# Relative-position bias rows: one product with eight output partitions, copied 128 times by the transfer to DRAM

## The reference

```python
bias = rel_bias[t5_bucket(sel_pos - q_pos[None, :, None])]
logits = logits + jnp.moveaxis(bias, 3, 1).astype(jnp.float32)
logits = jnp.where(valid[:, None], logits, -jnp.inf)
p = jax.nn.softmax(logits, axis=-1)
```

## Time and profile before

| | |
|---|---|
| three runs | 1038.37, 1040.26, 1038.22 us, median 1038.37 |
| profiled execution | span 1036.2 us from its first to its last instruction |
| TensorE busy | 1004.3 us, 97% |
| ScalarE, VectorE, GpSimd busy | 489.1, 621.5, 494.4 us |
| granted TensorE clock, mean | 0.996 of full |

### The profile page before, as it was taken

One profiled execution on the slowest core, in us unless ns is written; L12 is line 12 of the kernel. 1 busy time (PEld: TensorE's weight loads), 2 busy tenths in 40 slices (PEclk: granted clock), 3 DMA queues, 4 the chain that ended last, 5 costly groups with the idle time before them and its releaser, 6 DMA issues.

```text
span 1036.2 us, 18753 instructions
## 1 busy us (share of the span) xinstructions
PE 1004.3 (97%) x7590; PEld 921.0 (89%) x7590; DVE 621.5 (60%) x1221; ACT 489.1 (47%) x843; POOL 494.4 (48%) x331
## 2 busy tenths in 40 slices
PE   6999999999999999999999999899999999999996
PEld 5878997888899999997788899787888999999975
DVE  7579996879953200450765899978898320110137
ACT  6565336658866322222136633466788542222220
POOL 2425554535656534546324265555455464544540
PEclk9999999999999999999999999999999999999998
DMA  7521532101211425223243124301111222342312
GB/s 238 182 75 60 195 116 87 42 1 46 77 44 51 142 85 189 85 83 122 93 148 115 42 94 127 128 2 43 42 42 42 83 82 82 116 149 82 121 42 91
DMA packets 70105, 95.44 MB, mean 92 GB/s; under 512 B 4474, under 2 KB 61284, under 8 KB 69380
## 3 DMA queue, kind: packets, MB, share of 16 engines
q1 hardware_dynamic: 66068, 82.68, 23.9%
q0 software_dynamic: 3776, 11.50, 3.2%
q10 hardware_dynamic: 176, 0.07, 0.0%
HBM read 79.47 MB, written 14.78 MB: 91 GB/s over the span
## 4 chain that ended last, share of the span: by engine, by line
PE 81%; DVE 14%; issue 2%; ACT 2%; DMA 0%; POOL 0%; DVEq 0%; ACTq 0%; POOLq 0%
PE ps L559 36%; PE ps L915 10%; PE ps L866 10%; DVE attn L1520 3%; PE ps L781 3%; DVE top L1517 3%; PE ps L583 3%; PE ps L802 2%; PE ps L683 2%; PE ps L841 2%; PE ps L820 2%; PE ps L760 2%; PE ps L664 2%; PE ps L607 1%; DVE attn L1555 1%
## 5 line engine op out<-in xcount | busy, mean ns | idle before, releaser
L1759 POOL TENSOR_TENSOR w_lo<-raw,w_hi 128x1024 fp32r<-128x1024 f32 x115 | 282.0, 2452 | 390.3 <-ACT w_hi L966 390.1
L559 PE MATMUL ps<-xT_hi,w_hi 128*128 128x288 f32 x864 | 256.1, 296 | 0.0
L559 PE MATMUL ps<-xT_hi,w_lo 128*128 128x288 f32 x864 | 254.5, 295 | 0.0
L559 PE MATMUL ps<-xT_lo,w_hi 128*128 128x288 f32 x864 | 254.4, 294 | 0.0
L966 ACT ACTIVATE w_hi<-raw 128x1024 fp32r<-128x1024 f32 (+1 forms) x116 | 121.3, 1047 | 110.2 <-PE ps L559 71.2
L559 PEld LDWEIGHTS ps<-xT_hi,w_hi 128*128 128x128 f32 x864 | 162.1, 188 | 1.3 <-issue 1.1
L559 PEld LDWEIGHTS ps<-xT_lo,w_hi 128*128 128x128 f32 x864 | 162.1, 188 | 0.0
L559 PEld LDWEIGHTS ps<-xT_hi,w_lo 128*128 128x128 f32 x864 | 162.1, 188 | 0.0
L1720 DVE TENSOR_TENSOR qy<-qy,ps 128x576 f32<-128x576 f32 x32 | 24.1, 754 | 203.9 <-PE ps L559 203.9
L1074 ACT ACTIVATE qy<-ps,bias 128x576 f32<-128x576 f32 x33 | 24.5, 744 | 126.2 <-PE ps L559 126.1
L1851 POOL TENSOR_TENSOR attn<-attn 128x1024 f32<-128x1024 f32 (+1 forms) x24 | 54.2, 2260 | 59.1 <-DVE attn L1628 59.1
(11 more groups left out here) (227 smaller groups left out, 2327.1 us busy)
## 6 DMA issues: line engine op xcount, KB each, us to landing
raw<-in_w_in SPq DMA_DIRECT2D x44, 1024.0 KB, 4.9
raw<-in_w_out SPq DMA_DIRECT2D x8, 1024.0 KB, 4.9
x_kept<-x_nat SPq DMA_DIRECT2D x2, 2560.0 KB, 11.1
x_nat<-x_kept SPq DMA_DIRECT2D x2, 2560.0 KB, 11.8
raw<-in_w_proj_a SPq DMA_DIRECT2D x8, 512.0 KB, 3.5
raw<-in_w_proj_b SPq DMA_DIRECT2D x8, 512.0 KB, 4.5
x_nat<-in_x_prompt SPq DMA_DIRECT2D x4, 512.0 KB, 5.4
out<-stage POOLq DMA_DIRECT2D x8, 256.0 KB, 4.6
```

Of the source, the lines that this page charges most:

```text
L559: last = mm(out, a, b[:, HALF * half:HALF * (half + 1)], start=(k == 0 and i == 0), stop=(k == n - 1 and i == 2))
L1759: g.tensor_tensor(lo, src, hi.bitcast(f32), ALU.subtract).then_inc(s_lo, 1)
```

## The change

The table `rel_bias` itself (32 buckets by 8 heads) becomes the stationary operand. One product gives 8 partitions, one for each head, of 384 distances; the factor -1 goes into the one-hot matrix, on the host. `rel_wide`, its eight VectorE operations and its semaphore go, seven of the eight products and of the copies too. TensorE waits for the one copy where it waited for eight. The write to `scratch` reads the 8 partitions with a step of zero over 128 copies, so that `scratch` holds what it held before; it stands at the same place in SP's order.

```diff
@@ views
-        rows = view(r0, NH, REL)
+        rows = view(r0, REL)
-        rel_wide = stage[:, :, :].rearrange("p a n -> p (a n)")[:, 0:1024].rearrange("p (h n) -> p h n", h=NH)
@@ sync
                     if L == 0 and CHUNKS[c][0:2] == ("VA", 0):
-                        sp.wait_ge(s_relc, NH)
-                        sp.dma_start(scratch, rows[:, :, :]).then_inc(s_reld, 16)
+                        sp.wait_ge(s_relc, 1)
+                        of = rows[0:NH, :]
+                        sp.dma_start(scratch.rearrange("p h r -> h p r"),
+                                     bass.AP(of.tensor, of.offset, [list(of.ap[0]), [0, 128], [1, REL]])).then_inc(s_reld, 16)
@@ tensor
-            def rel_rows(h0):
-
-                if h0 == 0:
-                    pe.wait_ge(s_relw, NH)
-                    pe.wait_ge(s_trev, 1)
-                else:
-                    pe.wait_ge(s_relc, h0)
-                for h in range(h0, h0 + 4):
-                    mm(ps[:, 4 + h % 4, 0:REL], rel_wide[0:N_BUCKETS, h, :], onehot[0:N_BUCKETS, :],
-                       start=True, stop=True).then_inc(s_relp, 1)
+            def rel_rows():
+
+                pe.wait_ge(s_rel, 32)
+                pe.wait_ge(s_trev, 1)
+                mm(ps[0:NH, 4, 0:REL], rel_in[0:N_BUCKETS, :], onehot[0:N_BUCKETS, :],
+                   start=True, stop=True).then_inc(s_relp, 1)
...
-                    if L == 0 and u in (8, 9):
-                        rel_rows(4 * (u - 8))
+                    if L == 0 and u == 8:
+                        rel_rows()
                     if L == 0 and u == 10:
-                        pe.wait_ge(s_relc, NH)
+                        pe.wait_ge(s_relc, 1)
@@ scalar
-                    if L == 0 and u in (8, 9):
-                        for h in range(4 * (u - 8), 4 * (u - 8) + 4):
-                            act.wait_ge(s_relp, h + 1)
-                            act_f(rows[:, h, :], ps[:, 4 + h % 4, 0:REL], ACT.Copy).then_inc(s_relc, 1)
+                    if L == 0 and u == 8:
+                        act.wait_ge(s_relp, 1)
+                        act_f(rows[0:NH, :], ps[0:NH, 4, 0:REL], ACT.Copy).then_inc(s_relc, 1)
@@ vector
-                    dve.wait_ge(s_rel, 32)
-                    for h in range(NH):
-                        v.tensor_scalar(rel_wide[0:N_BUCKETS, h, :], neg_one[0:N_BUCKETS, :], 1.0,
-                                        rel_in[0:N_BUCKETS, h:h + 1], ALU.mult, ALU.mult).then_inc(s_relw, 1)
@@ constants
     one[half - 1] -= 1.0
+    one *= -1.0
```

More of the change, by code:

```diff
@@ L252, in build @@
         shift_in = view(18432, D)
-        rel_wide = stage[:, :, :].rearrange("p a n -> p (a n)")[:, 0:1024].rearrange("p (h n) -> p h n", h=NH)
-        neg_one, before_f, admit_f = (const[:, n, :] for n in range(3))
+        before_f, admit_f = (const[:, n, :] for n in (1, 2))
         gb = qy[:, 0:4, :].rearrange("p m t -> p (m t)")[:, 0:2 * D].rearrange("p (a n) -> p a n", a=2)
@@ L261, in build @@
         s_rel = sem("rel_arrived")
-        s_relw = sem("rel_widened")
         s_relp = sem("rel_rows_done")
```

## The result

The changed kernel took 1045.42 us (median of four runs, 1043.93 to 1045.89), against 1038.49 for the kernel before (four runs, 1038.22 to 1040.26): a ratio of 1.0059, with a 95% interval of 1.0042 to 1.0075. It is slower by 6.9 us, where 1040.9 was forecast and 1044.0 was the end of the range. The profiled execution is the one of 1045.89, with a span of 1044.1.

The account below looks back on a forecast made before the run. TensorE was taken as the bound (busy 97%, 81% of the chain). Saved products -4.88, idle TensorE +5.7 and slower clock +1.7 gave +2.5 us on 1038.4, so 1040.9 us; range 1033.3 to 1044.0.

Parts of the forecast that it names:

- TensorE, 4.88 us saved: Bias products between dense units 8, 9 and 10: one product for eight saves 2.02 us in the first block, 2.86 in the second.
- VectorE and ScalarE hidden, no reserve at the logits: Their removed work gains nothing; logits 4.88 us earlier, at 155.81, just meet VectorE's last mask ending at 155.7.
- rival 2: At the first logits: no stall, but VectorE's last mask runs beside a GpSimd w_lo, about 1.6 us late; 1034.9 us, chance 0.10.
- The write's own time, 29 us: Write to scratch from 8 partitions: 29 us taken, between bounds of 3.7 and 58, running from 109.6 to 138.6.
- The halvings by the number of partitions: Write rate from 64 to 8 partitions: three halvings possible, giving 7.3, 15, 29 or 58 us; two were taken.
- VA 1 behind the write: Weights for units 16 and 17, behind the write on SP's queue and shared DMA engines: land at 141.8.
- TensorE idle, 5.7 us: Ahead of unit 16: it would start at 145.45, waiting for late weights, and not at 139.75.
- The clock, 1.7 us: After TensorE's idle time: one stretch of 3.4 us at half speed costs 1.7 us, bounds 0 and 3.4.
- Rival 3: At unit 16: the stall comes but TensorE's clock stays; 1039.2 us, chance 0.20.
- bias_near and QA 0 hidden: Loads issued after the write: bias_near lands about 149 with little lost; QA 0's weights feed unit 18, 13.8 us on.
- Stage stores, hidden: GpSimd's stores of stage tiles share the DMA engines, but cost nothing, as a tile is written again only two units later.
- Rival 1: The write to scratch is little or not limited by its partitions (up to 23 us): 1033.5 us, chance 0.18 together with another rival.

Follow-up runs that it names:

- the transposes: The changed kernel with 68 identity transposes that nothing reads, on TensorE ahead of its wait for unit 16: 1042.94 us (7 runs), ratio 1.0045.

## Why the prediction was wrong in size and right in kind

- **TensorE, 4.88 us saved:** right. The block costs 0.82 where it cost 2.86 and 0.84 was worked out, the second is gone; and with the write made fast, 4.6 to 4.8 us of it reach the end.
- **VectorE and ScalarE hidden, no reserve at the logits:** right. With no stall the mask ends 0.4 us before the logits are taken, and rival 2 (a w_lo beside the last mask that makes VectorE late) did not come: that mask took the same 0.32 us. This was in part luck of timing. The w_lo did stand beside the mask, but began at 155.56, 0.06 us behind it (heads on 128 partitions), so that a w_lo that begins first was never tried.
- **The write's own time, 29 us:** this is the term that was mis-sized. It took 32.7, and landed at 142.66 - 0.46 = 142.2 where 138.6 was forecast. The halvings by the number of partitions were the wrong picture, though they came near for eight neighbours: the rate goes by which partitions are read, about 50 GB/s from 0 to 7 and 201 from eight that lie four apart. What was missing on top is the sharing: GpSimd's stores, which I named and priced at nothing, took 1.8 to 2.6 us of the write's time, and 1.1 more stay without a shown cause.
- **VA 1 behind the write:** right in kind. It landed 3.7 us after the write where I took 3.2, so at 145.9 instead of 141.8. I named the SP queue and the shared DMA engines; the runs with the write on ScalarE's queue show that the hold-up does not need the queue, and the packets that it strikes the half of the weights that shares the write's eight engines.
- **TensorE idle, 5.7 us:** 9.6 measured. The difference, 3.9, is the 4.1 of VA 1. From the weights to unit 16 it took 149.95 - 146.38 = 3.57 us, where 3.65 was worked out.
- **The clock, 1.7 us:** 2.4 by the two units' times, of which the transposes took back 2.1. I took one low stretch of 3.4 us beginning with the work; it lasted 10.2 us, from 144.4 to 154.7, of which 5.5 fell in the idle time and cost nothing, and 4.7 at half speed cost 2.35, all of what unit 16 took longer. The price lies inside the bounds of 0 to 3.4, but by a stretch three times as long that began in the idle time: the size came out near by luck. Rival 3, a stall with no loss of clock, is wrong.
- **bias_near and QA 0 hidden:** right here. They are hidden only as long as VA 1 is what is late: with VA 1 ahead of the write, QA 0 behind bias_near made a stall of 10.3 us.
- **Stage stores, hidden because "a tile is written again only two units later":** wrong, two units are too few. A store that took a median of 4.1 us in the kernel with a fast write took 11.8 in this stretch, and ScalarE stood 9.4 us at the tile. TensorE did not pay for that wait, since the weights came later still.

With the terms as measured the prediction's own sum gives -4.9 + 9.6 + 2.4 = +7.1, against +6.9 by the medians. Of the miss of 4.5 us (1045.4 against 1040.9), 3.9 come from the time at which VA 1 lands and 0.7 from the clock; of the 3.9 nearly all is the write's own length, the rest VA 1's 3.7 behind it in place of 3.2. So the step that failed is the write's own time, 32.7 us and not 29; the 32 at which the range ended is passed by that term alone. The range erred in that it took 26 to 32 us for the write and nothing for what else used the same engines.

Rival 1 gave 1033.5 for a write that isn't limited by its partitions; with the write read from 128 partitions, and from eight that lie four apart, the kernel took 1033.85 and 1033.65.

## What to carry to other kernels

Before a transfer is made to replicate few rows with a step of zero, look at which partitions it reads, not only at its bytes: eight neighbours gave an eighth of the rate of 128 partitions, and eight that lie four apart gave half, for a few zero columns in the stationary operand that cost TensorE nothing. A slow transfer delayed what was issued behind it on each of the queues tried (SP's weights behind a write of SP or ScalarE, GpSimd's stores), so price it by the next transfers that engines wait for, those of other engines among them, and let each term of that sum carry the others' traffic. To save engine time and lose it to a later weight is a bad trade; the same saving with a write that stays short is worth 4.6 to 4.8 us here.

## What the runs showed of the hardware that I had not expected

- Partitions of a read, same bytes and same number of partitions: 48 to 52 GB/s from 0 to 7, 113 from every second of 0 to 14, 201 from every fourth of 0 to 28; 402 from all 128.
- The DMA engines' share stays at 0.44 to 0.53 for the slow ones: eight of sixteen are held and the others are free, and still a transfer of 1 MB on another queue takes 28 to 31 us instead of 5, since half of it waits for the held ones.
- The granted clock stayed at 1.00 for 4 us of idle TensorE (140.3 to 144.4), then was 0.50 for 10.2 us, 4.7 of them with TensorE at work again. Work that nothing uses held it at 1.00 and took 2.1 us off unit 16.
